# A two-block transformer forward pass: gate residues on another engine, 512-column token slots, late loads on another queue, first gather in halves, last load in pieces

## What is computed

```
aff = softmax(h @ w_router)                     # 256 x 16
g, idx = top_k(aff.T, 32)                       # 32 tokens for each expert
xe = h[idx]
ye = (silu(xe @ w_gate) * (xe @ w_up)) @ w_down * g   # 1024x2048, 1024x2048, 2048x1024
out = rms_norm(x + scatter_add(ye), norm_f_g)
```

## Time and profile before

| | us |
|---|---|
| median of three runs | 1527.29 (1526.12 to 1528.37) |
| the profiled execution | 1527.02 |
| its span | 1524.7 |
| TensorE busy | 1114.1 (73%) |
| VectorE busy | 401.8 (26%) |
| ScalarE busy | 315.5 (21%) |
| POOL busy | 54.9 (4%) |
| loads issued by SP | 508.57 MB |

### The profile page before, as it was taken

How to read it: one execution, slowest core, us unless ns; L and a number is a source line. 1 busy time by engine, 2 the same in 40 slices (tenths; PEclk the granted TensorE clock), 3 DMA queues, 4 the chain that set the end, 5 groups by cost and what they waited for, 6 DMA issues and landing times.

```text
span 1524.7 us, 17121 instructions
## 1 busy us (share of the span) xinstructions
PE 1114.1 (73%) x7544; PEld 674.8 (44%) x7544; DVE 401.8 (26%) x729; ACT 315.5 (21%) x541; POOL 54.9 (4%) x50
## 2 busy tenths in 40 slices
PE   6889999998999879965656656667555557555555
PEld 4866898987999778511122111113111113111111
DVE  2447664655768664200000000000000000000001
ACT  3246553544645544000000000000000000000001
POOL 0020000000014300000000000000000000000000
PEclk9999999999999989987888887878778889788787
DMA  9989456552763247899999999999999999999996
GB/s 366 293 282 376 136 177 194 192 192 69 221 230 119 84 193 303 371 438 428 429 435 428 434 432 429 433 430 432 429 431 432 430 435 426 434 432 426 437 428 264
DMA packets 87619, 516.42 MB, mean 339 GB/s; under 512 B 6415, under 2 KB 63226, under 8 KB 71802
## 3 DMA queue, kind: packets, MB, share of 16 engines
q1 hardware_dynamic: 82512, 508.57, 82.1%
q10 hardware_dynamic: 4106, 4.57, 0.9%
q0 software_dynamic: 928, 2.20, 0.6%
HBM read 514.12 MB, written 1.07 MB: 338 GB/s over the span
## 4 chain that ended last, share of the span: by engine, by line
DMA 52%; PE 39%; DVE 4%; issue 2%; ACT 1%; POOL 1%; ACTq 1%; SPq 0%; DVEq 0%; POOLq 0%
DMA expert_ring<-in_w_up_e 19%; DMA expert_ring<-in_w_gate_e 17%; DMA expert_ring<-in_w_down_e 15%; PE PS L517 8%; PE PS L518 8%; PE PS L519 8%; PE PS L976 5%; PE PS L1007 2%; DMA ring<-in_w_ada 2%; PE PS L511 1%; DVE wR L367 1%; PE PS L595 1%; PE PS L950 1%; PE PS L563 1%; POOL arena L1922 1%
## 5 line engine op out<-in xcount | busy, mean ns | idle before, releaser
L976 PE MATMUL PS<-expert_ring,xeT 128*32 128x512 f32 x2048 | 320.5, 784 | 234.3 <-DMA expert_ring<-in_w_up_e 126.6
L976 PEld LDWEIGHTS PS<-expert_ring,xeT 128*32 128x32 f32 x2048 | 76.3, 139 | 475.6 <-issue 217.3
L1552 DVE TENSOR_TENSOR expert_rows<-expert_rows,PS 128x512 f32<-128x512 f32 x16 | 11.0, 688 | 806.4 <-PE PS L976 806.4
L1007 PE MATMUL PS<-expert_ring,expert_rows 128*32 128x512 f32 x992 | 145.0, 739 | 90.4 <-DMA expert_ring<-in_w_down_e 88.3
L517 PE MATMUL PS<-hR,wR 128*128 128x256 f32 x632 | 183.3, 290 | 10.6 <-DVE wR L367 10.6
L359 ACT ACTIVATE wR<-ring 128x1024 fp32r<-128x1024 f32 (+2 forms) x144 | 144.3, 1051 | 216.1 <-PE PS L519 207.5
L518 PE MATMUL PS<-hR,wR 128*128 128x256 f32 x632 | 181.6, 287 | 0.0
L519 PE MATMUL PS<-hR,wR 128*128 128x256 f32 x632 | 181.5, 287 | 0.0
L367 DVE TENSOR_TENSOR wR<-ring,wR 128x1024 fp32r<-128x1024 f32 x128 | 150.8, 1221 | 105.3 <-ACT wR L359 105.2
L517 PEld LDWEIGHTS PS<-hR,wR 128*128 128x128 f32 x632 | 124.4, 197 | 12.5 <-issue 8.2
L518 PEld LDWEIGHTS PS<-hR,wR 128*128 128x128 f32 x632 | 124.3, 197 | 0.0
(11 more groups left out here) (266 smaller groups left out, 1101.2 us busy)
## 6 DMA issues: line engine op xcount, KB each, us to landing
expert_ring<-in_w_up_e SPq DMA_DIRECT2D x32, 4096.0 KB, 43.2
expert_ring<-in_w_gate_e SPq DMA_DIRECT2D x31, 4096.0 KB, 43.0
expert_ring<-in_w_down_e SPq DMA_DIRECT2D x30, 4096.0 KB, 44.4
ring<-in_w SPq DMA_DIRECT2D x32, 1024.0 KB, 5.3
ring<-in_w_in SPq DMA_DIRECT2D x31, 1024.0 KB, 6.2
ring<-in_w_ada SPq DMA_DIRECT2D x24, 1024.0 KB, 9.2
ring<-in_w_out SPq DMA_DIRECT2D x8, 1024.0 KB, 8.5
expert_ring<-in_w_gate_e SPq DMA_DIRECT2D x2, 2048.0 KB, 9.3
```

What stands on the lines that cost most here:

```text
L976: mm = nc.tensor.matmul(PS[32 * j:32 * j + 32, kind // 2, :], xeT[:, e // GROUP % 2, k, own], w[:, j // 2, j % 2, :, :], start=(k == 0), s ...
L1007: mm = nc.tensor.matmul(PS[32 * at:32 * at + 32, 3, :], hidT[:, c % 4, 2 * q + c // 4, :], w[c][:, 512 * half:512 * (half + 1)], start=(q ...
```

## The change

1. All residues are VectorE's. In the unit loop it does that of slot `G_GATES2 + u + 2` at the end of iteration u, so that the first two slots of the up-projection are also done there. ScalarE rounds the second gate slot after its last eviction of the mixer projection instead of before it.
2. Slots of `tokens_still` (w_in 4 and 5; six of the mixer projection), w_out and w_out_2 hold 512 columns by half of the rows. Two slots make one 128x512 tile for each token tile; VectorE evicts the first and ScalarE the second, both after the second slot.
3. SP issues the late loads: relb, the constants, sinks and lam before w_in slot 6; the router, gain_rows and mgate before slot 8; bmg (four loads), b2, G1 and G2 before the third slot of w_ada's second part.
4. Norm 4 takes its squares and its multiplication in halves of 512 columns; ScalarE multiplies the second half.
5. The first gather is cut: four K chunks, unit 0, four K chunks, unit 1.
6. The second half of the last unit is issued as pieces of 1 MB, 512 KB and 512 KB with a semaphore each.

```diff
-BY_POOL = [g for g in SPLIT if G_GATES2 <= g < G_UP]
-BY_DVE = [g for g in SPLIT if g not in BY_POOL]
+MIX_TOKENS = (4, 5, 10, 11, 12, 13)
...
 SP, in the loop over slots:
+                if g == G_WIN + 6:
+                    sp.dma_start(relb[:, :], A["rel_bias"]).then_inc(consts_in, 16)
+                    sp.dma_start(const[:, P:C_END], A["shape_constants"][:, P:C_END]).then_inc(consts_in, 16)
...
+                if g == G_WIN + 8:
...
+                if g == G_ADA12 + 2:
+                    sp.wait_ge(bmg_set, 1)
...
 SP, the last unit:
+                if u == EXPERTS * UNITS_EACH - 1:
+                    sp.dma_start(expert_ring[:, FILL[b], 0:4 * D], src[:, 0:4 * D]).then_inc(unit_loaded[b], 16)
+                    sp.wait_ge(pairs_used, 2 * unit_of(n - BUFFERS) + 2)
+                    for sem, first, last in zip(tail_loaded, (4, 6, 7), (6, 7, 8)):
+                        part = slice(first * D, last * D)
+                        sp.dma_start(expert_ring[:, FILL[b], part], src[:, part]).then_inc(sem, 16)
+                    continue
 TensorE:
+            def tokens_half(g, half, o, t, seeded=False):
+                w = parts(g, 4)
+                for k in range(4):
+                    mm = product(o, [x[:, k, :] for x in w], [hR[:, part, 4 * half + k, t * P:(t + 1) * P] for part in range(2)],
+                                 "tokens", half == 0 and k == 0 and not seeded, half == 1 and k == 3, onto=True)
+                return mm
...
-                if i in (4, 5, 10, 11, 12, 13):
-                    tokens_still(G_MIX2 + i, i % 4)
+                if i in MIX_TOKENS:
+                    if i % 2 == 0:
+                        pe.wait_ge(mix_out[1], (i - 4) // 2 + 1)
+                    tokens_still(G_MIX2 + i, i % 2, i % 4 - i % 2)
...
-            gather(0)
+            gather(0, range(KD // 2))
             for e in range(EXPERTS):
                 for kind in range(4):
+                    if e == 0 and kind == 1:
+                        gather(0, range(KD // 2, KD))
...
+                        elif u == EXPERTS * UNITS_EACH - 1 and c >= 4:
+                            if c != 5:
+                                pe.wait_ge(tail_loaded[(c - 4) // 2 + c // 7], 16)
 VectorE, mixer projection:
-                dve.wait_ge(slots_used, used(G_MIX2 + i))
+                if i in MIX_TOKENS:
+                    residue_slot(dve, V, G_MIX2 + i + 2)
+                dve.wait_ge(slots_used, used(G_MIX2 + (i + 1 if i in MIX_TOKENS else i)))
...
-                if i + 2 < N_MIX2:
+                if i not in MIX_TOKENS:
                     residue_slot(dve, V, G_MIX2 + i + 2)
 VectorE, unit loop and behind it:
+                if u < 2 * MH:
+                    residue_slot(dve, V, G_GATES2 + u + 2)
...
-            residue_slot(dve, V, G_UP)
-            residue_slot(dve, V, G_UP + 1)
 VectorE, norm 4:
-                norm_tile(N4, t, sums)
+                dve.wait_ge(root_set, root_of(N4, t))
+                V.reciprocal(stats[:, N4, 4 + t:5 + t], stats[:, N4, 2 + t:3 + t]).then_inc(fourth_factor, 1)
+                dve.wait_ge(fourth_factor, t + 1)
+                V.tensor_scalar(work[:, t, 0:512], PS[:, 4 + 2 * t, :], stats[:, N4, 4 + t:5 + t], None, ALU.mult).then_inc(normed, 1)
 ScalarE:
-            late_loads()
...
-                round_slot(act, G_MIX2 + i + 2)
+                if i < N_MIX2 - 1:
+                    round_slot(act, G_MIX2 + i + 2)
...
+            round_slot(act, G_MIX2 + N_MIX2 + 1)
...
-            act.wait_ge(wout2_first, 1)
-            root(N4, 0, sums, work)
-            act.wait_ge(slots_used, PRELUDE)
-            root(N4, 1, sums, work)
+            act.wait_ge(slots_used, used(G_WOUT2 + 1))
+            for t in range(NT):
+                half_square(N4, t, PS[:, 4 + 2 * t, :])
+            for t in range(NT):
...
+                root_rest(N4, t, PS[:, 5 + 2 * t, :])
+                act.wait_ge(fourth_factor, t + 1)
+                N.activation(work[:, t, 512:D], PS[:, 5 + 2 * t, :], ACT.Copy, scale=stats[:, N4, 4 + t:5 + t]).then_inc(fourth_normed, 1)
 POOL:
-            pool.wait_ge(normed, 2 * T3 + 2)
-            for g in BY_POOL:
-                residue_slot(pool, G, g)
```

More of the change, by code:

```diff
@@ L357, in round_slot @@
                 eng.wait_ge(slots_used, used(SPLIT[n - 2]))
-            for piece in pieces(g):
+            for piece in pieces():
                 nc.scalar.activation(halves(g, 0)[:, piece], slot(g)[:, piece], ACT.Copy).then_inc(slot_rounded, 1)
@@ L362, in residue_slot @@
             n = SPLIT.index(g)
-            sem = slot_split_pool if g in BY_POOL else slot_split_dve
             arrived(eng, g)
-            for i, piece in enumerate(pieces(g)):
+            for i, piece in enumerate(pieces()):
                 eng.wait_ge(slot_rounded, 2 * n + i + 1)
                 by.tensor_tensor(halves(g, 1)[:, piece], slot(g)[:, piece], halves(g, 0)[:, piece], ALU.subtract)\
-                    .then_inc(sem, 1)
+                    .then_inc(slot_split, 1)
         def after(g, k=2):
@@ L419, in k8, with k4 @@
             return slot(g).rearrange("p (k n) -> p k n", k=KD)
+        def k4(g):
+            return slot(g).rearrange("p (k n) -> p k n", k=4)
         loads = []
@@ L425, in build_program @@
         for i in range(N_WIN):
-            loads.append((k8, w_in[:, :, 256 * i:256 * (i + 1)]))
+            if i in (4, 5):
+                loads.append((k4, w_in[:, 4 * (i - 4):4 * (i - 3), 1024:1536]))
+            else:
+                loads.append((k8, w_in[:, :, 256 * i:256 * (i + 1)]))
         for r in (1, 2):
@@ L430, in build_program @@
         for i in range(N_WOUT):
-            loads.append((k8, w_out[:, :, 256 * i:256 * (i + 1)]))
+            loads.append((k4, w_out[:, 4 * (i % 2):4 * (i % 2) + 4, 512 * (i // 2):512 * (i // 2 + 1)]))
         for half in range(2):
@@ L439, in build_program @@
         gate_cols0 = DIFF0 + 3 * MW
-        for c in mix_cols + [gate_cols0 + 256 * i for i in range(N_GATES2)]:
-            loads.append((k8, w_in2[:, :, c:c + 256]))
+        for i, c in enumerate(mix_cols + [gate_cols0 + 256 * i for i in range(N_GATES2)]):
+            if i in MIX_TOKENS:
+                c -= 256 * (i % 2)
+                loads.append((k4, w_in2[:, 4 * (i % 2):4 * (i % 2) + 4, c:c + 512]))
+            else:
+                loads.append((k8, w_in2[:, :, c:c + 256]))
         for half in range(2):
             for w in (up_a, up_b):
-                loads.append((lambda g: slot(g).rearrange("p (k n) -> p k n", k=4), w[:, :, 512 * half:512 * half + 512]))
+                loads.append((k4, w[:, :, 512 * half:512 * half + 512]))
         for i in range(N_WOUT2):
-            loads.append((k8, w_out2[:, :, 256 * i:256 * (i + 1)]))
+            loads.append((k4, w_out2[:, 4 * (i % 2):4 * (i % 2) + 4, 512 * (i // 2):512 * (i // 2 + 1)]))
         assert len(loads) == PRELUDE
@@ L566, in raw_channels, with tokens_still @@
                 return mm
-            def tokens_still(g, bank):
-                w = parts(g, KD)
+            def tokens_still(g, half, bank):
                 for t in range(NT):
-                    mm = tokens_out(PS[:, bank, t * 256:(t + 1) * 256], w, slice(0, 256), t)
+                    mm = tokens_half(g, half, PS[:, bank + t, :], t)
                 mm.then_inc(slots_used, 1)
@@ L580, in turn_tile @@
                 for k in range(KD):
+                    if n == T4 and k == 4:
+                        pe.wait_ge(fourth_normed, t + 1)
                     mm = turn(PS[:, base + 2 * t + k // 4, (k % 4) * P:(k % 4 + 1) * P],
@@ L939, in _, with gather @@
             mm.then_inc(rank_cols, 1)
-            def gather(group):
+            def gather(group, ks=range(KD)):
                 if group == 0:
@@ L946, in gather @@
                     pe.wait_ge(sel_rest_set, 1)
-                for k in range(KD):
+                for k in ks:
                     o = PS[:, 2 + k // 4, (k % 4) * P:(k % 4 + 1) * P]
```

102 lines of the change are left out of this document (48 added, 54 removed).

## The result

The changed kernel takes 1506.4 us in the median of four runs (1503.96 to 1508.08), the kernel before 1527.8 beside it; the ratio is 0.9858 with a 95% interval from 0.9837 to 0.9878, some 21 us faster. Run a second time it took 1508.7 beside 1528.4 (0.9868, 0.9851 to 0.9886). Forecast were 1502, in a range from 1496 to 1511: the result lies inside it, 4.4 us above the forecast. Against the kernel before beside it, which took 1527.8 and not 1527.3, 3.9 us of the expected gain did not come; in the two profiled executions 6.3 did not.

The account below looks back on a forecast made before the run. The kernel was taken as a prelude to about 602 us, a fixed-rate expert weight stream and a 12.6 us tail. Savings of 20.3 (prelude), 3.7 (after 601.9) and 1.2 (tail) made 25.2: 1502 us, range 1496 to 1511.

Parts of the forecast that it names:

- Late loads, 7.1: Prelude, w_in: issuing the late loads on SP removes ScalarE's issue stall and starts the attention 7.1 us earlier.
- Slots, 1.1 + 1.8 + 1.1: 512-column token slots need less product time: 1.1 us saved in w_out, 1.8 in the mixer projection, 1.1 in w_out_2.
- Unit loop, 6.8: Attention unit loop: gate residues on VectorE end the stretching beside POOL and bring it near TensorE's bound, 6.8 us saved.
- the 5.2 us of waits: Unit loop: VectorE's remaining idle, 4.4 us at the last units and 0.8 at the head, added to its 64.0.
- Up-projection, 2.4: Start of w_up: its first two residues are already done, so TensorE's wait shortens by 2.4 us.
- Gather in halves, 3.1: After the prelude: unit 0 starts after half the gather, so the weight stream restarts 3.1 us earlier.
- Rival 4: Weight stream: restart comes early but a new hole between units 6 and 7 loses 3.7 us, 1506 us; chance 0.10.
- just in time: Weight stream: unit 6 alone carries the queue for 9.7 us until unit 7 is issued; 0.1 us lost at most.
- Fourth norm, 0.6: Before the gather: VectorE's 1.28 us multiplication of tile 1 is shared with ScalarE in halves, 0.6 us saved.
- Tail, 1.2: After the last landing: four products remain instead of 16 once the last 512 KB piece is apart, 1.2 us saved.
- the first theory: First gather, forecast for the follow-ups: halves would pay 3 us, but TensorE's 0.78 us stop brings the low clock.

Follow-up runs that it names:

- its own experiment: Fourth norm scaled by VectorE alone in one pass per tile, against the changed kernel; 1509.5 us, ratio 0.9874 to the kernel before.
- the gather with spare products: Three 128x256 TensorE products that nobody reads added behind each half of the first gather, against the changed kernel; 1506.3 us, ratio 0.9856 to the kernel before.

## Why the prediction was right, and where it fell short

The result lies in the range, and most terms came as priced; but two were well off, and two errors the other way (the tail, and idle time that no term held) covered part of that. So the total is nearer than the working deserved.

**Late loads, 7.1: right.** The logits came 6.85 earlier, and undoing the edit alone costs 8.7 at the same place. SP's side cost nothing that shows, as costed: TensorE does not wait in w_in, and from the logits to w_out's first product it is 40.4 us in both kernels. The Trainium skill, "DMA: Bandwidth & Descriptors", section "Issuing engines are not separate DMA queues", calls the sequencer's time usually small; here it was a stall of 8.5 to 10.5 us on ScalarE with a rounding behind it, and the measurement decides.

**Slots, 1.1 + 1.8 + 1.1: right.** w_out 1.0 (42.06 to 41.08, with a low spell of the clock in both), w_out_2 1.1, the mixer's products 75.52 to 74.23, 1.3. The half microsecond missing there is more than made up by the idle ahead of unit 0's scores (2.68 to 0.78), which no term held.

**Unit loop, 6.8: the step that failed.** The mechanism stood: no stretched operation is left, and the dummy work on GpSimd shows that its presence alone makes them. The Trainium skill, "SBUF — State Buffer", section "Who interferes with whom", is narrower than the prediction told it. It names VectorE instructions in a two-port mode, and those with two inputs in SBUF beside a GpSimd instruction that reads SBUF, and says that one with at most one SBUF input outside the two-port modes does not contend. The traces agree: 33 instructions that read PSUM kept their length beside GpSimd, and eight from SBUF to SBUF stretched by 0.35 to 3.16 us. (One of the eight in the kernel before ends 0.28 us after GpSimd's piece, not within 0.15.) The size was off: 3.45. I had reasoned from two sums, VectorE's 64.0 and TensorE's 66.1 us of work, and allowed waits only at both ends of the loop. Undisturbed units do run so, at 8.3 us each. But when the mLSTM units give way to the differential ones, ScalarE holds a rounding behind exponentials that wait for VectorE, which waits for the rounding of the slot: 2.04 + 2.24, and a slot at the lower clock. Changing the order gave 2.9 of the missing 3.35, 2.2 of it by the order itself. The term that was mis-sized is the 5.2 us of waits (4.4 at the end of the loop and 0.8 at its head): it lacks those of 2.04 and 2.24 us in mid-loop.

**Up-projection, 2.4: right,** 2.2 (91.07 to 88.91 with only w_up's residues moved). It starts as VectorE's last hR residue ends (531.15 and 531.10), as the prediction had it. Within w_up's products the clock cost 1.0 that was not in the sum.

**Gather in halves, 3.1: the other step that failed.** It gave 0.15 in the table, 0.3 beside the whole gather. Rival 4 described half of it: unit 7's load is late behind the second half. The other half is the clock: at the lower level unit 0 takes 5.64 us, and unit 6's load goes out only 1.1 earlier. I had followed the first transfer that moves and dismissed the second as "just in time", by sums at the upper clock. In the trace of before the whole gather had been one unbroken row of products; I did not ask what the clock would do once a stop of 0.78 us was put into it, nor what it was already doing there: 0.69 was granted from 620 to 624 us, with TensorE busy all 4.0.

**Fourth norm, 0.6: right,** 0.4 to 0.6 by its own experiment. **Tail, 1.2: too small.** It gave 2.4: 1.4 from twelve products fewer behind the landing (1.05 us for 2.46), 1.8 from the scatter (1.99 for 3.78) and 0.8 given back behind it. I had left the clock out, so what the scatter adds to the gain is luck. With the last load in halves again the sixteen products lie at the lower level (3.48 us) and the scatter at the upper: the longer piece is paid for at one or the other, behind a stop of 2.6 to 2.9 us that small pieces avoid.

**The clock.** Five profiled kernels do the same up to the gather (the changed one twice, the gather whole, the gather with spare products, the last load in halves), and the profiles fall into two kinds: w_up in 24.4 to 24.5 or 25.5 us, and the 32 router products in 3.7 or 4.6, with 15.9 to 16.1 or 17.9 to 18.0 us from the prelude's last product to the gather. Two have the shorter values and three, the changed kernel's own among them, the longer ones in both. That is 1.0 and 1.9 us of its shortfall, owed to no edit. Not all of it is a net loss, though: the two with the shorter values came later to the scores of unit 0 (446.8 and 448.0 us, the three 444.1 to 445.7), with more of the lower clock between the logits and w_out (0.92 and 0.93 for 0.96 to 1.00), and all five begin the gather between 600.2 and 602.8 us. It also means that the first theory (the 0.78 us stop brings the low clock) isn't shown: with the halves unedited unit 0 ran at either level, and with the whole gather the granted clock was 0.70 from 604 to 608 while TensorE was busy all 4.0 us. Spare products went with the upper level in all three profiles that had them ahead of unit 0 or w_up. For w_up that says more: only the two with them have 23.1 us, all twelve others 24.4 to 25.5.

## To carry to other kernels

When a queue is emptied of one stall, walk one full change of phase in all the queues that hand over to each other: two sums of work that fit don't show a cycle of waits. A transfer that moves earlier helps only as far as the next ones keep up, so list the issue times of the three behind it, at both levels of the clock. And judge single edits by stretches of the profile between two fixed rows: the whole time scattered by 3 to 9 us, these stretches by about 0.1 outside the clock's spells, and by 0.8 to 4 with them. So compare two profiles only where the granted clock of the stretch is the same.

## What the runs showed of the hardware

- GpSimd's 128x512 passes stretch VectorE's work with no data in common: 10.7 us more busy time on the same 215 instructions beside 40.4 us of GpSimd. It is the work from SBUF to SBUF that stretches (a 128x256 scale of 0.35 us to 3.50, a 128x4 operation of 0.16 to 2.43); what reads PSUM kept its length in 33 cases of 33.
- A spell of the lower clock costs what stands in it: 1.5 us in the w_out stage (39.54 to 41.08), 0.9 on the 32 router products, 2.0 on an expert unit (3.64 to 5.64). Whether it came differed between kernels that were the same up to there; what decides it is open.
- One 128x256 product in f32 takes 0.22 us for each of its two instructions at the upper level, so 18 of them fill 7.93 us.
